# First norm by a matrix of ones, a logarithm and an exponential, rows multiplied ahead of their modulations, and modulation units placed by arrival

## What is computed

```python
y = x * rsqrt(mean(x * x, axis=-1) + EPS) * g        # rmsnorm, EPS = 1e-6, 1024 channels
z = y * (1.0 + scale) + shift                        # modulate: m[0] is shift, m[1] is scale
m = split(silu(c) @ w_ada + b_ada, 9)                # one set for latent, one for context tokens
gate, up = split(z @ w_in, 2)                        # 2 x 2816 columns
h = h + 0.5 * m[2] * ((silu(gate) * up) @ w_out)
```

## Time and profile before

| what | value |
|---|---|
| median of 3 runs | 1557.17 us (1557.15 to 1559.31) |
| the profiled execution | 1556.19 us, its span 1554.3 us |
| PE busy | 1532.4 us, 99% of the span, 8822 instructions |
| DVE, ACT, POOL busy | 67%, 44%, 10% of the span |
| PE's share of the chain that ended last | 95% |
| first slice of 39 us: PE, DVE, ACT, DMA busy | 80%, 50%, 40%, 90% |
| fourth slot's first product | 45.29 us |

### The profile page before, as it was taken

One profiled execution on the slowest core, in us unless ns is written; L12 is line 12 of the kernel. 1 busy time (PEld: TensorE's weight loads), 2 busy tenths in 40 slices (PEclk: granted clock), 3 DMA queues, 4 the chain that ended last, 5 costly groups with the idle time before them and its releaser, 6 DMA issues.

```text
span 1554.3 us, 22125 instructions
## 1 busy us (share of the span) xinstructions
PE 1532.4 (99%) x8822; PEld 1312.5 (84%) x8822; DVE 1047.9 (67%) x1294; ACT 679.2 (44%) x1105; POOL 157.5 (10%) x188
## 2 busy tenths in 40 slices
PE   8999999999999999999999999999999999999997
PEld 6888888888878888888888898888888896999997
DVE  5777874784868577874378577875358769975553
ACT  4434433333684343433233352433333359664453
POOL 0011110022000201101002200011002211000011
PEclk9999999999999999999999999999999999999999
DMA  9577764674422257663367437664257525455562
GB/s 370 203 210 202 208 186 130 210 211 130 140 82 69 95 176 211 198 187 102 114 202 220 128 124 215 204 211 122 95 189 225 168 91 157 150 190 197 191 205 94
DMA packets 77228, 264.64 MB, mean 170 GB/s; under 512 B 9424, under 2 KB 9680, under 8 KB 76112
## 3 DMA queue, kind: packets, MB, share of 16 engines
q1 hardware_dynamic: 69456, 250.80, 49.1%
q0 software_dynamic: 7680, 12.59, 5.1%
HBM read 247.62 MB, written 1.05 MB: 160 GB/s over the span
## 4 chain that ended last, share of the span: by engine, by line
PE 95%; ACT 1%; DVE 1%; DMA 1%; issue 0%; SPq 0%; POOL 0%; DVEq 0%
PE bank L484 86%; PE bank L612 2%; PE bank L606 2%; PE bank L608 2%; DMA ada_head<-head_w 1%; PE bank L747 1%; PE bank L772 1%; PE bank L749 1%; PE bank L748 1%; PE bank L561 0%; ACT w_hi L901 0%; PE bank L783 0%; PE bank L500 0%; PE bank L537 0%; DVE w_lo L1198 0%
## 5 line engine op out<-in xcount | busy, mean ns | idle before, releaser
L901 ACT ACTIVATE w_hi<-raw 128x1024 fp32r<-128x1024 f32 x317 | 336.1, 1060 | 714.0 <-PE bank L484 697.1
L1198 DVE TENSOR_TENSOR w_lo<-raw,w_hi 128x1024 fp32r<-128x1024 f32 x317 | 389.5, 1230 | 311.1 <-ACT w_hi L901 310.7
L484 PE MATMUL bank<-z_hi,w_hi 128*128 128x512 f32 (+2 forms) x1480 | 534.4, 361 | 2.2 <-DVE w_lo L1198 1.8
L484 PE MATMUL bank<-z_lo,w_hi 128*128 128x512 f32 (+2 forms) x1480 | 531.8, 359 | 0.0
L484 PE MATMUL bank<-z_hi,w_lo 128*128 128x512 f32 (+2 forms) x1480 | 531.7, 359 | 0.0
L484 PEld LDWEIGHTS bank<-z_hi,w_hi 128*128 128x128 f32 x1480 | 277.8, 188 | 52.7 <-issue 5.7
L484 PEld LDWEIGHTS bank<-z_hi,w_lo 128*128 128x128 f32 x1480 | 277.9, 188 | 42.6
L484 PEld LDWEIGHTS bank<-z_lo,w_hi 128*128 128x128 f32 x1480 | 277.9, 188 | 41.4
L484 PE MATMUL bank<-h_hi,w_hi 128*128 128x512 f32 (+1 forms) x770 | 265.4, 345 | 0.0
L484 PE MATMUL bank<-h_lo,w_hi 128*128 128x512 f32 (+1 forms) x770 | 264.9, 344 | 0.0
L484 PE MATMUL bank<-h_hi,w_lo 128*128 128x512 f32 (+1 forms) x770 | 264.8, 344 | 0.0
(11 more groups left out here) (177 smaller groups left out, 1376.7 us busy)
## 6 DMA issues: line engine op xcount, KB each, us to landing
raw<-weights SPq DMA_DIRECT2D x320, 512.0 KB, 4.2
ada_raw<-ada_w SPq DMA_DIRECT2D x128, 512.0 KB, 4.2
ada_head<-head_w SPq DMA_DIRECT2D x8, 1024.0 KB, 18.4
up_acc<-up_acc POOLq DMA_DIRECT2D x20, 256.0 KB, 6.6
down_acc<-down_acc POOLq DMA_DIRECT2D x12, 256.0 KB, 6.2
up_acc<-up_acc POOLq DMA_DIRECT2D x40, 64.0 KB, 5.6
res<-x_t SPq DMA_DIRECT2D x4, 512.0 KB, 5.1
xc_swapped<-xc SPq DMA_DIRECT2D x16, 128.0 KB, 2.4
```

Source lines behind the costliest of these rows:

```text
L484: m = pe.matmul(bank[:, to], w, x[:, k, at], start=start and i == 0, stop=stop and i == 2, skip_group_check=True)
L901: act.activation(w_hi[:, r, weights_at(s)], raw[:, r, :], ACT.Copy).then_inc(hi_ready, 1)
L1198: dve.tensor_tensor(w_lo[:, r, weights_at(s)], raw[:, r, :], w_hi[:, r, weights_at(s)].bitcast(F32), ALU.subtract).then_inc(lo_ready, 1)
```

## The change

Five things change in the head, and nothing behind it but the counts of some semaphores.

1. The sums of squares: TensorE takes all eight rows, each as one float32 product of 512 columns with a stationary matrix of ones (`ones` broadcast to 128 x 128), so that the sum of all channels stands on every partition at once. The one-column sums, VectorE's additions, the variance, GpSimd's power, the spread products and the second set of throwaway products go.
2. The factor: ScalarE makes the logarithm of the mean plus epsilon into `scr` and the exponential of -1/2 of it into a bank. The table set for both is loaded ahead of the squares; the exponential of `softplus` then needs no load of its own.
3. The rows: VectorE multiplies x by the factor alone (`scaled`, 512 columns into `head_sq`), which needs no modulation, and rows are made ahead of the turns. When row k is turned, ScalarE applies gain and shift in place (two halves, each with an operand of its own for scale and for bias) and copies to `z_hi`; VectorE makes `z_lo` from the two as one piece of 512. The first weights' split stands ahead of the first `z_lo`.
4. The order on TensorE of units and sweeps is written out anew.
5. `params` is issued ahead of x, and the Silus of the conditioning vector stand ahead of the squares.

The diff, cut to its core:

```diff
# SP
+            sp.dma_start(par[:], params).then_inc(par_in, 16)
             for i in range(X_PIECES):
...
-            sp.dma_start(par[:], params).then_inc(par_in, 16)
# TensorE
+            def first_sums():
+                for d in range(KD):
+                    pe.wait_ge(sq_ready, d + 1)
+                    m = pe.matmul(po[0][:], ones[:, 0:1].to_broadcast([P, P]), head_sq[:, d, :], start=d == 0, stop=d == KD - 1)
+                m.then_inc(head_sum, 1)
...
                     head_unit(1)
                     swept(0, 0)
+                    swept(0, 1)
                     head_unit(2)
                     swept(1, 0)
-                    swept(0, 1)
                     swept(1, 1)
+                    swept(0, 2)
                     head_unit(3)
+                    swept(1, 2)
                     swept(2, 0)
-                    swept(0, 2)
-                    for step in range(3, KD + len(banks) - 1):
-                        swept(step - 2, 2)
-                        swept(step - 1, 1)
-                        if step < KD - 1:
-                            head_unit(step + 1)
-                        swept(step, 0)
+                    swept(2, 1)
+                    head_unit(4)
+                    swept(2, 2)
+                    head_unit(5)
+                    swept(3, 0)
+                    swept(3, 1)
+                    head_unit(6)
+                    swept(3, 2)
+                    swept(4, 0)
+                    head_unit(7)
+                    swept(4, 1)
+                    swept(4, 2)
+                    for k in range(5, KD):
+                        for q in range(len(banks)):
+                            swept(k, q)
...
             throwaway(WARM_UP, p_ada, T)
             throwaway(2 * WARM_UP, p_ada)
-            for d in range(SUMS_DIRECT):
-                first_sums(d)
-            throwaway(WARM_UP, p_ada, T)
-            throwaway(3 * WARM_UP, p_ada)
-            norm_sums(0, 0)
-            norm_sums(0, 1)
+            first_sums()
             pe.wait_ge(cvec_ready, 1)
             head_unit(0)
-            norm_spread(0, 0)
-            norm_spread(0, 1)
# ScalarE (the two Silus of the conditioning vector and the table load now ahead of the squares)
+            def head_norm():
+                act.wait_ge(hid_ready, HID0)
+                act.wait_ge(head_sum, 1)
+                act.activation(scr[:, 1, :], po[0][:], ACT.Ln, bias=eps, scale=1.0 / D).then_inc(log_ready, 1)
+                act.wait_ge(log_ready, 1)
+                act.activation(po[1][:], scr[:, 1, :], ACT.Exp, scale=-0.5).then_inc(inverse_ready, 1)
+                def head_row(k):
+                    act.wait_ge(zt_ready, z_piece(0, k, 1))
+                    act.wait_ge(head_mods, 2 * k + 2)
+                    for s in range(2):
+                        act.activation(head_sq[:, k, COLS[s]], head_sq[:, k, COLS[s]], ACT.Identity,
+                                       bias=n_shift[:, 0, k, s:s + 1], scale=n_gain[:, 0, k, s:s + 1]).then_inc(head_z, 1)
+                    act.wait_ge(head_z, 2 * k + 2)
+                    act.activation(z_hi[:, k, :], head_sq[:, k, :], ACT.Copy).then_inc(z_hi_ready, 2)
+                for k in range(KD):
+                    if k < SIDE:
+                        split_hi(k, k)
+                    head_row(k)
...
+                split_hi(SIDE, SIDE)
+                act.activation(warm[:], ones[:, 0:1], ACT.Silu)
# VectorE
+            def head_norm():
+                def scaled(k):
+                    if k == 0:
+                        dve.wait_ge(inverse_ready, 1)
+                    dve.tensor_tensor(head_sq[:, k, :], res[:, k, :], po[1][:], ALU.mult).then_inc(zt_ready, 2)
...
+                def z_low(k):
+                    dve.wait_ge(z_hi_ready, z_piece(0, k, 1))
+                    dve.tensor_tensor(z_lo[:, k, :], head_sq[:, k, :], z_hi[:, k, :].bitcast(F32), ALU.subtract).then_inc(z_ready, 2)
+                scaled(0)
+                scaled(1)
+                turn(0)
+                split_lo(0, 0)
+                z_low(0)
+                turn(1)
+                scaled(2)
+                split_lo(1, 1)
+                z_low(1)
+                scaled(3)
+                lam_abs()
+                scaled(4)
+                turn(2)
+                split_lo(2, 2)
+                z_low(2)
+                scaled(5)
+                turn(3)
+                scaled(6)
+                z_low(3)
+                turn(4)
+                z_low(4)
+                scaled(7)
+                for k in range(5, KD):
+                    turn(k)
+                    z_low(k)
+                split_lo(3, 3)
```

More of the change, by code:

```diff
@@ L310, in halves, with roots @@
             return sum(streams(dft(i)) for i in range(n))
+        def roots(n):
+            return halves(n) - halves(1)
         def ring_piece(at, t):
@@ L520, in norm_sums @@
                     return
-            def first_sums(d):
-                pe.wait_ge(sq_ready, d + 1)
-                for s in range(2):
-                    for j in range(2):
-                        m = 2 * s + j
-                        pe.matmul(ss_bank(0, s)[:, j:j + 1], head_sq[:, d, m * P:(m + 1) * P], ones[:, 0:1],
-                                  start=d == 0 and j == 0, stop=False, skip_group_check=True)
+            def first_sums():
[3 more added lines that the diff above has]
+                m.then_inc(head_sum, 1)
             def norm_spread(n, s):
-                pe.wait_ge(rstd_ready, halves(n) + s + 1)
+                pe.wait_ge(rstd_ready, roots(n) + s + 1)
                 spread(spread_bank(n, s), s).then_inc(bcast_done, 1)
@@ L961, in norm @@
                             split_hi(base + 3, 3)
-                        if n == 0 and s == 1:
-                            for q in {0: (1,), 1: (2,), 6: (3,)}.get(k, ()):
-                                split_hi(q, q)
-                        if n == 0 and s == 1 and k == 4:
-                            act.wait_ge(lam_ready, 1)
-                            act.activation(lam_t[:, 1, :], lam_t[:, 0, :], ACT.Exp, scale=-1.0).then_inc(lam_ready, 1)
                     act.activation(warm[:], ones[:, 0:1], ACT.Silu)
@@ L1162, in _ @@
             act.activation(warm[:], ones[:, 0:1], ACT.Silu)
-            for d in range(KD):
-                if d * X_PIECES % KD == 0:
-                    act.wait_ge(x_in[d * X_PIECES // KD], 16)
-                square(d, 0)
             act.wait_ge(par_in, 16)
@@ L1171, in _ @@
                            ACT.Silu).then_inc(cvec_ready, 1)
-            split_hi(0, 0)
-            norm(0, 0)
+            load_log_and_exp()
+            for d in range(KD):
+                if d * X_PIECES % KD == 0:
+                    act.wait_ge(x_in[d * X_PIECES // KD], 16)
+                square(d, 0)
+            head_norm()
             for l in range(DEPTH):
@@ L1236, in norm @@
             def norm(n, base):
                 w = dft(n)
-                if n == 0:
-                    first = SUMS_DIRECT
-                    for d in range(first + 1, KD):
-                        dve.wait_ge(sq_ready, d + 1)
-                        if d > first + 1:
-                            dve.wait_ge(head_sum, d - first - 1)
-                        dve.tensor_tensor(scr[:, 2, :], head_sq[:, first, :] if d == first + 1 else scr[:, 2, :], head_sq[:, d, :],
-                                          ALU.add).then_inc(head_sum, 1)
@@ L1248, in variance @@
                 def variance(s):
-                    dve.wait_ge(ss_done, halves(n) + s + 1)
+                    dve.wait_ge(ss_done, roots(n) + s + 1)
                     dve.tensor_scalar(tok[:, 2 * s:2 * s + 2], ss_bank(n, s)[:, 0:2], 1.0 / D, EPS,
@@ L1272, in norm @@
                     variance(0)
-                if n == 0:
-                    variance(1)
                 if split_rows(n) == (6, 7):
@@ L1298, in scaled @@
                     if n == 3 * DEPTH - 1:
-                        dve.wait_ge(inverse_ready, 1)
+                        dve.wait_ge(inverse_ready, 2)
                     else:
-                        dve.wait_ge(bcast_done, halves(n) + s + 1)
+                        dve.wait_ge(bcast_done, roots(n) + s + 1)
                     dve.scalar_tensor_tensor(scr[:, k % 3, COLS[s]], res[:, k, COLS[s]], n_gain[:, n, k, s:s + 1],
@@ L1702, in prep_gate @@
                 at = ADA_ORDER.index((l, 3 * i + 2))
[L1703 removed]
+                pool.wait_ge(mods_ready, 16 * (at + 1))
                 a = at * KD
```

81 lines of the change are left out of this document (28 added, 53 removed).

## The result

The changed kernel took **1560.37 us** (median of 14 runs, 1559.49 to 1561.56), the kernel before 1557.13 in the same comparison (14 runs, 1555.61 to 1559.31). The ratio is 1.0022 with a 95% interval of 1.0015 to 1.0030: slower by 3.2 us, at the edge of the 0.2% that was set as the limit of "no change". The forecast was 1558.8 in 1556.0 to 1561.3. So the sign and the range held, and the centre was 1.6 us too low.

A forecast was written before the change was run, and what follows sets the result against it. TensorE's own work was taken as the bound, so time falls only with its waits. +1.3 at the fourth slot and +0.4 at the fifth, less 0.1 for the clock, gave +1.6 us: 1558.8, range 1556.0 to 1561.3.

The forecast's parts named there:

- one of its own signs: On TensorE: the forecast is wrong if products at 20 to 26 us stand 0.45 us apart.
- Sums: Sums of squares on TensorE: 16 instructions 0.43 us apart from 7.10, issued by 14.1, done by 14.25.
- cover of 3.2 us: Ahead of the squares on ScalarE: `params`, two Silus and a table load would have to cost 3.2 us to show.
- Factor and first row: ScalarE and VectorE: factor at 15.65 us, then first row and split; first sweep at 20.0, 1.6 us later.
- Second slot and third unit: Slot 1's `w_lo` at 22.3 us; unit 2, queued behind that sweep, at 23.2 instead of 20.05; TensorE 2.5 behind.
- Rest: TensorE from 23.2 us: 22.45 of work plus 0.7 of waits; fourth slot +1.1 to +1.9 us, +1.3 taken.
- the standstill: Unit 5 on TensorE stood still 0.57 us before its last two products; its return puts the mark at 47.2, not 46.4.
- The mark: Start of the fourth weight slot on TensorE, 45.29 us before; its shift was taken to go to the end.
- What is late next: Fifth slot waits for the first hidden row behind VectorE's split and softplus chain: +0.4 us, or nothing if the mark is later.
- The rival of the clock: TensorE's clock falls in the gap before the first sweep: +1.3 to +2.8 us on top, 1560.1 to 1561.6; chance 0.22.
- The early factor: Sums at 0.23 us an instruction end about 11, first sweep 17.5, mark 44: -1.2 us, 1556.0; chance 0.15.

The follow-up runs named there:

- e2: The changed kernel with `params` issued behind x again and the Silus and table load behind the squares; +3.9 us against the kernel before, ratio 1.0024.
- e9: e8 with `params` issued behind x again and the Silus and table load behind the squares; +1.2 us against the kernel before, ratio 1.0006.
- e5: The changed kernel with throwaway products in three gaps: around unit 1 and between the first sweeps of slots 0 and 1; +2.7 us against before, ratio 1.0019.
- e4: The kernel before with only the new order of units and sweeps on TensorE; +3.5 us against the kernel before, ratio 1.0020.
- e6: e3 with throwaway products in the two gaps around unit 1; +3.8 us against the kernel before, ratio 1.0026.
- e1: The changed kernel with throwaway products in the two TensorE gaps around unit 1; +3.0 us against the kernel before, ratio 1.0021.
- e12: The changed kernel with squares rounded to fp32r and summed with fp32r ones, one instruction a row; +3.6 us against the kernel before, ratio 1.0021.
- e11: e10 with squares rounded to fp32r and summed with fp32r ones, one instruction a row; +1.2 us against the kernel before, ratio 1.0004.
- e10: e9 with two sweeps between units 5 and 6 and two between 6 and 7; +0.7 us against the kernel before, ratio 1.0005.
- e8: The changed kernel with unit 2 ahead of slot 1's sweep, a fill ahead of slot 0 and VectorE's list rearranged; +1.9 us against before, ratio 1.0011.
- e3: The changed kernel with the old order of units and sweeps on TensorE; +3.5 us against the kernel before, ratio 1.0021.

## Why the prediction was right or wrong

By one of its own signs the forecast was wrong: products at 20 to 26 us were not to stand 0.45 apart, and from 20.98 on they stood 0.38 to 0.59 apart. The measured +3.2 lies above its own +0.3 to +2.8, and inside the range only through the upper end that was drawn out for the fallen clock. The steps, in their order:

**Sums.** The pace of 0.43 us an instruction held (twelve in 5.42 us, less the tail), and the start (7.09). The end was 14.84 and not 14.25, because the cover of 3.2 us that was claimed for the squares was not there: the second piece of x landed at 8.7 us, and the squares of six rows ran from 8.73 to 12.35 instead of ending near 9.9. Costing `params` and the landings at nothing was wrong by 0.4 us of these 0.6 (the fifth sum instruction started at 9.42, where the pace would have had it at 9.04; the rest is the clock's start); e2 and e9, with `params` behind, have the sums unbroken.

**Factor and first row.** Logarithm 0.69, exponential 0.60 and the pair with two operands 1.09 were forecast as 0.69, 0.60 and 1.11. From the sums' end to the first sweep it took 6.14 us against 5.72 forecast, the rest being handovers between engines of about 0.1 each that were counted as 0.04. First sweep 20.98 for 20.0.

**Second slot and third unit.** Right in place and size: VectorE did difference, turn 1, a row and then the split, slot 1's sweep waited for it, and unit 2 was queued behind. In e5, where x landed sooner and the clock stayed, the forecast's times stand almost to the digit: 19.95 for 20.0, 22.27 for 22.3, 23.17 for 23.2. The first of these is in part luck: e5's sums ended at 13.78 instead of 14.25, and the way from there took 6.17 instead of 5.72. That this queue alone is worth the whole loss is not shown: e4, which lost as much, has the whole new order and a fallen clock.

**Rest.** Here the forecast failed in one term. It left open whether the standstill comes again and took +1.3 between +1.1 without it and +1.9 with it. It came, and larger: unit 6 took 39.89 - 37.52 = 2.37 us, 1.34 too many, in the changed kernel, and e5, whose unit 2 is on time, has the fourth slot at 47.84, where 46.4 was forecast without and 47.2 with it (its unit 6 lost 1.5). The mark of the changed kernel's profile, 50.13, is 3.5 us over the 46.6 taken: 1.0 from the first sweep, 0.7 and 1.4 from the low clock (from slot 1's sweep to unit 2 it took 24.89 - 23.31 = 1.58 instead of 0.9, and unit 2 with the next sweep, which ended at 28.13, 3.24 instead of 1.8), 1.1 from the standstill (1.34, of which the forecast had taken in 0.2), less the 0.7 of waits that no longer showed.

**What is late next.** The fifth slot waits for the first hidden row behind the softplus chain, as forecast: from fourth to fifth slot 5.79 us instead of 5.44, +0.35 for +0.4. Nothing else behind the mark changed: 4.84 + 0.35 is the span's 5.2.

**The rival of the clock.** It happened in the profiled run, but not as its condition said: unit 1 came 2.0 us later than taken (17.60, its block landed at 17.47), so two waits of 1.74 and 2.28 us stood where one of 3.3 was expected, and the clock fell at 21.20, not before 20. The measured median lies in its 1560.1 to 1561.6. The forecast gave it 0.22 and chose the other case; by the trace this choice was wrong. The rule that the prediction took from the Trainium skill (TensorE: Matmul & The Clock Gate, section "Why this matters for your kernels"), that gaps between bursts cost the clock, agrees with the trace in kind; the trace has no one long gap, but the two waits with a unit of 1.03 us between them.

Its price was set at +1.3 to +2.8. By the account above it was 0.7 and 1.4 less the 0.7 of hidden waits, some 1.4 us; by the medians, taking the fall away gave back 0.6 us in e5 and nothing in e6. So the price lies at the lower end of what was set or below it, and the intervals do not say more. The mean granted clock of the 14 runs (0.995 or 0.996, in the profiled run 0.996) fits a fall in each of them but does not show it: of the 93 runs of the kernel before that stand beside e1 to e12, 41 have 0.995 or 0.996 as well, where its profiled run, with no fall in the head, has 0.998. These 41 took 0.25 to 0.6 us longer in the median than the others of their set, which hints at a small price; no trace shows where the clock was low in them.

**The early factor** did not occur; e11 and e12 made it by hand, and it gave nothing at the end. The clock fell early in both (14.01 and 10.93), so what it would give with the clock whole is not shown.

The sum, then: the queues ahead of unit 2 and the later rows cost what was forecast; the size of the standstill, the late landings and the fall of the clock did not stand in it. That e10, which keeps the new norm and mends order, clock, landing and spacing together, stands at +0.7 us (ratio 1.0005, 0.9996 to 1.0014, against 1.0015 to 1.0030) shows that most of the 3.2 us lies in these terms together. Their shares are not measured: the steps on the way (+2.7 in e5, +1.9 in e8, +1.2 in e9, +0.7 in e10) are each smaller than an interval. Of the 0.9 us that e10's fourth slot is still late, all lies behind unit 2, which starts at 20.03 as before (20.05): it lost 0.91 + 0.58 + 0.59 us there in two standstills and a row, the kernel before 0.57 + 0.41. No version was measurably faster than the kernel before.

## What to carry to other kernels

Ask of each edit what stands behind it in the same engine's queue: a product that must wait for a split, put ahead of a unit whose data had landed, held that unit up by 3.8 us in e4. A norm and an order of sweeps are tuned to each other, so try each alone; here each alone lost 3.5 us. And where a profile shows idle time named "issue" inside a run of small, dense instructions, count TensorE's instructions from there on in steps of some 256: there lie the next places where it can happen (not each of them stops). Slower instructions ahead of such a place let the block arrive, but they gain only if they are work that had to be done anyway; in e10 most of the standstill went over into a wait for a row.

## What the runs showed of the hardware

TensorE's instructions arrived in blocks of 16 KB, some 256 instructions. Where TensorE reached the end of a block less than some 1.3 to 1.5 us after the next packet had ended, it stood still until then, 0.57 to 1.55 us in 14 cases, each inside a unit of 64 loads and 64 products. Why a block comes when it does was not tried. In e9 the next packet began 5.5 and 3.9 us after TensorE had gone on at 22.04 and 30.11, while weight transfers kept the DMA engines fully busy (share 1.01), and 1.1 us after it had gone on at 36.46, when they no longer did (0.60 from 36 to 38 us). That would fit a fetch that waits behind the weights, which no run shows.

A transfer of 156 KB ahead of x lengthened the landing of the second piece of x: 4.3 to 4.6 us in the seven traces without it in front, 4.9 to 7.0 in the seven with it (7.0 in the changed kernel, 5.0 in e1, 6.5 in e3), so that this term differs from run to run.

The clock fell with fills in only two of the three waits (e1) and stayed with all three filled (e5); in e12 it fell among the sums, at 10.93 us, after waits of 1.23 and 0.27 us between them. Before, it stayed whole with waits of 1.76 and 0.64 us in the same stretch; in e11 it fell at 14.01, in a wait of 2.67 that followed one of 1.45.
